# Third expert matrix in 16 KB runs, with an expert's hidden units dealt to the two halves in pairs

## The reference

```python
hdn = jax.nn.silu(xf @ w1[e]) * (xf @ w3[e])        # 1024 -> 512 hidden units
acc = acc + combine[:, e:e + 1] * (hdn @ w2[e])     # 512 -> 1024
```

## Time and profile before

| | |
|---|---|
| median of 3 runs | 716.95 us (716.07 to 717.56) |
| profiled execution, own time | 716.73 us |
| its span, first to last instruction | 715.0 us |
| PE busy | 609.8 us (85%) |
| weight loads (PEld) / DVE / ACT / POOL busy | 420.6 / 306.9 / 181.8 / 158.4 us |
| DMA traffic | 235.99 MB, mean 330 GB/s over the span |
| granted TensorE clock, mean | 0.961 |
| `into_hidden` (L694): matmul instructions | 1952 + 160, mean 396 and 407 ns |
| `down` (L715): matmul instructions | 464 + 64, mean 596 and 654 ns |
| issues of the expert matrices | 96 of 2048 KB |

### The profile page before, as it was taken

How to read it: one execution, slowest core, us unless ns; L and a number is a source line. 1 busy time by engine, 2 the same in 40 slices (tenths; PEclk the granted TensorE clock), 3 DMA queues, 4 the chain that set the end, 5 groups by cost and what they waited for, 6 DMA issues and landing times.

```text
span 715.0 us, 10596 instructions
## 1 busy us (share of the span) xinstructions
PE 609.8 (85%) x4220; PEld 420.6 (59%) x4220; DVE 306.9 (43%) x787; ACT 181.8 (25%) x287; POOL 158.4 (22%) x181
## 2 busy tenths in 40 slices
PE   5999999999999999889877987988788777877771
PEld 5999999878775556446444544554344435453440
DVE  4462485517577133353442353342434251433244
ACT  3323313302111313223232323322232121223130
POOL 1000000000000414244235224332341322233142
PEclk9999999999989999999999999899999999999996
DMA  9952133834496999999999999999999999999950
GB/s 250 282 184 90 45 118 105 339 135 190 152 392 250 390 418 420 417 416 417 422 416 421 413 422 416 422 416 421 422 418 421 415 422 420 425 415 418 404 223 21
DMA packets 45738, 235.99 MB, mean 330 GB/s; under 512 B 13667, under 2 KB 18275, under 8 KB 28712
## 3 DMA queue, kind: packets, MB, share of 16 engines
q1 hardware_dynamic: 32287, 220.92, 76.6%
q0 software_dynamic: 12544, 11.71, 4.9%
q10 hardware_dynamic: 857, 2.67, 0.9%
HBM read 237.69 MB, written 30.20 MB: 375 GB/s over the span
## 4 chain that ended last, share of the span: by engine, by line
PE 34%; issue 19%; DMA 17%; SPq 15%; POOL 9%; DVE 5%; ACT 1%; POOLq 0%; DVEq 0%; ACTq 0%
PE ps L534 14%; SPq L402 9%; PE ps L591 7%; DMA tenth_block<-in_w 6%; DMA blocks<-in_w 6%; PE ps L694 6%; SPq L406 5%; PE ps L715 2%; POOL out L1085 2%; POOL out L1081 2%; POOL prev L1077 2%; POOL first_outputs L1073 2%; DMA first_outputs<-ye,first_row 2%; DMA x_tok<-in_x_prompt 1%; DMA prev<-first_outputs,final_row 1%
## 5 line engine op out<-in xcount | busy, mean ns | idle before, releaser
L694 PE MATMUL ps<-blocks,ln 128*64 128x256 f32 x1952 | 233.5, 396 | 53.6 <-DMA blocks<-in_w 32.4
L694 PEld LDWEIGHTS ps<-blocks,ln 128*64 128x64 f32 x1952 | 157.0, 143 | 130.2 <-issue 57.2
L715 PE MATMUL ps<-blocks,hT 128*64 128x512 f32 x464 | 105.7, 596 | 6.0 <-DMA blocks<-in_w 5.8
L1077 POOL DMA_INDIRECT prev<-first_outputs,final_row x32 | 34.9, 1091 | 246.7 <-DMA first_outputs<-ye_more,first_row 119.3
L715 PEld LDWEIGHTS ps<-blocks,hT 128*64 128x64 f32 x464 | 32.8, 137 | 59.8 <-issue 48.5
L798 ACT ACTIVATE ln<-ps 128x512 f32<-128x512 f32 (+1 forms) x38 | 19.9, 572 | 112.2 <-PE ps L682 89.0
L1494 DVE SCALAR_TENSOR_TENSOR h_rows<-silu,slot_gate,ps 128x256 f32<-128x256 f32 x33 | 15.7, 477 | 69.0 <-PE ps L694 68.9
L1499 DVE COPY hT<-ps 128x256 f32<-128x256 f32 x33 | 13.9, 422 | 71.1 <-PE ps L703 71.1
L534 PE MATMUL ps<-xT_high,w_in_high 128*128 128x288 f32 x256 | 41.4, 305 | 0.9 <-DVE xT_low L1187 0.9
L981 ACT ACTIVATE std<-rstd,eps 128x1 f32<-128x1 f32 x32 | 9.4, 295 | 125.3 <-DVEq L1523 125.2
L534 PE MATMUL ps<-xT_low,w_in_high 128*128 128x288 f32 x256 | 39.5, 297 | 0.0
(11 more groups left out here) (232 smaller groups left out, 789.6 us busy)
## 6 DMA issues: line engine op xcount, KB each, us to landing
blocks<-in_w SPq DMA_DIRECT2D x87, 2048.0 KB, 36.5
tenth_block<-in_w SPq DMA_DIRECT2D x9, 2048.0 KB, 37.9
blocks<-in_w_in SPq DMA_DIRECT2D x3, 2048.0 KB, 10.5
blocks<-in_w_out SPq DMA_DIRECT2D x2, 2048.0 KB, 7.8
x_tok<-in_x_prompt SPq DMA_DIRECT2D x4, 512.0 KB, 5.2
blocks<-in_w_in SPq DMA_DIRECT2D x4, 512.0 KB, 11.3
first_outputs<-in_x_prompt SPq DMA_DIRECT2D x4, 512.0 KB, 8.7
x_rows<-x_tok ACTq DMA_DIRECT2D x4, 512.0 KB, 2.7
```

What stands on the lines that cost most here:

```text
L694: mm = pe.matmul(ps[64 * g:64 * g + 64, bank, 0:FH], x, w[:, k, g * FH:(g + 1) * FH], start=(k == 0), stop=(k == KD - 1))
L715: mm = pe.matmul(ps[64 * g:64 * g + 64, BY, :], hT[:, k % 2, k // 2 * SLOTS:(k // 2 + 1) * SLOTS], w[:, k, g * DH:(g + 1) * DH], start=(k ...
L1077: return g.indirect_dma_start(out=prev[w], out_offset=None, in_=first_rows[:, :], in_offset=rows_at(idx), bounds_check=last_row, oob_is_er ...
```

## The change

It has two sides that need each other. `load_out` gives partition p the rows 4p to 4p+3 of `w2`, one run of 16 KB. For these rows to meet their units, the 512 units are dealt to the halves by pairs: half g takes the units 4q + 2g and 4q + 2g + 1 for q = 0 to 127. In `into_hidden` the moving operand of half g is thus 128 pairs of neighbouring fp32 values, 8 bytes used and 8 bytes skipped, in place of 256 values in a row. What PE writes to PSUM, the number and order of all instructions, the transposes and `down` stay as they are, on every engine; SP has as many DMA issues as before.

```diff
@@ -403,8 +403,7 @@
             def load_out(b, e):
                 src = w2[e] if isinstance(e, int) else w2[bass.DynSlice(e, 1)].rearrange("e f d -> (e f) d")
-                sp.dma_start(out_block(b).rearrange("p (g c) d -> p g c d", g=2),
-                             src.rearrange("(g p c) d -> p g c d", g=2, c=KF // 2)).then_inc(block_loaded[b], 16)
+                sp.dma_start(out_block(b), src.rearrange("(p c) d -> p c d", c=KF)).then_inc(block_loaded[b], 16)
@@ -685,14 +684,14 @@
             def into_hidden(kind, b, loads, seq, i):
                 done, bank = (h1_done, B1) if kind == "w1" else (h_done, B3)
-                w = in_block(b)
+                w = in_block(b).rearrange("p k (q g c) -> p k g q c", g=2, c=2)
...
                     for g in range(2):
-                        mm = pe.matmul(ps[64 * g:64 * g + 64, bank, 0:FH], x, w[:, k, g * FH:(g + 1) * FH],
-                                       start=(k == 0), stop=(k == KD - 1))
+                        mm = pe.matmul(ps[64 * g:64 * g + 64, bank, 0:FH].rearrange("s (q c) -> s q c", c=2), x,
+                                       w[:, k, g, :, :], start=(k == 0), stop=(k == KD - 1))
```

## The result

| | before | changed |
|---|---|---|
| median, same chip, 7 runs each | 717.56 us | 721.97 us |
| range of the runs | 716.07 to 719.52 | 720.16 to 723.05 |
| ratio, 95% interval | | 1.0058 [1.0040, 1.0076] |
| profiled execution, own time | 716.73 us | 722.03 us |
| its span | 715.0 us | 720.3 us |

What follows compares the result with a forecast made beforehand. Block loads on the DMA engines were taken as the bound, the last `w3` landing setting the end: 716.73 - 2.4 (DMA) + 0 (PE) = 714.3, plus 0.2 for the median, 714.5 us; own range 713.3 to 715.3, 8 in 10 711.9 to 717.3.

Steps and rivals of the forecast that it cites:

- The failed step: POOL's gathers: small packets wait 0.3 us longer behind a 16 KB packet; taken as 0, 0.3 us at the end without cover.
- The chain over POOL is off the path: At the end, DVE waited 0.22 us for the last gather, the last `w2` having landed by then; cost taken as 0.
- 19.6 us for silu: Mid-kernel, PE's waits for ACT were said to come behind a late block, since silu uses what PE had just finished.
- 78 us are free: Expert part: PE busy 407.92 of 486 us, about 15 us unavoidable, so extra call time up to about 1 us fits.
- The DMA term: `w2` loads on the DMA engines: fewer, larger packets save 90 ns a load, 27 loads, 2.4 us; bounds 0 to 5.9.
- p = 0: `into_hidden` (L694): p is a call's extra time from gapped moving rows, taken as 0; upper end 3.4 us.
- the rival of a small p: L694 calls take 0.3 to 1 us longer, hidden in PE's gaps except 3p: 715.4 to 717.5 us; chance 0.07.
- The rival on the other side: L694 in every pair: gapped rows make PE the bound, near 880 us at half speed, 766 at p = 1.7; chance 0.11.

Runs made afterwards that it cites:

- gaps-only: Changed kernel with `w2` loaded as before in two runs of 8 KB, leaving only the gapped moving rows: 717.67 us, ratio 1.0012.
- DMA-only: Kernel before with only the changed `load_out` (`w2` in one 16 KB run), moving rows without gaps: 722.51 us, ratio 1.0083.
- all-8 KB: Kernel before with every `w1` and `w3` load also in two runs of 8 KB, no gaps: 720.34 us, ratio 1.0058.
- the round shortened: Kernel before with second norm one tile later and POOL's load of `prev` after store t, waiting only for store t-1: 721.90 us, ratio 1.0072.
- the fetch first: Changed kernel with POOL's fetch of a later pair's tokens issued ahead of the load of `prev`: 721.56 us, ratio 1.0078.
- later norm: Second norm of each tile handled one tile later: on the changed kernel ratio 1.0025, on the kernel before 0.9998, on DMA-only 1.0003.
- last edit: As the round shortened, but the last three tiles in the old order: changed kernel 1.0082, kernel before 0.9989, DMA-only 1.0061.
- late-tiles kernel: Kernel before with the whole change (16 KB `w2` runs, gapped rows) only from tile 20 on: 716.16 us, ratio 0.9981.

## Why the prediction was wrong, step by step

- **The failed step** is "A 16 KB packet holds its engine for 0.3 us longer, and the small packets of POOL's gathers wait behind it", with "The chain over POOL is off the path [...] I take 0". The mechanism was named, and priced once, at the end. But it acts all along the queue: 12.7 us in place of 11.5 for each store that POOL waits for, two a pair, and a pair was 29.2 us long instead of 27.1. Whether POOL was off the path was read from one row of the last 25 us; until 492 us PE ran at POOL's pace, and the earlier trace rows had shown it: its 19.6 us for silu were put down to late blocks. Cut at 485 us, that stretch has 17.9 of them, and no wait for a block, in its first part, and all of the 24.1 us for blocks in the second (below). The gaps-only, DMA-only and all-8 KB kernels show the step, the last of them in the other direction.
- **The spare time of PE.** "78 us are free" counted idle time as if it lay anywhere. The nine pairs up to 492 us need 51 loads, not 54, since the crowded expert's two tiles, 8 and 9, share one set of matrices (tile 9 is the added one, not the last tile, `E`). At 5.42 us a load these are 276 us, and at POOL's pace PE took them in 244: it won the 32 us by which it had begun behind the loads. The changed kernel begins some 3.5 us further behind (first `w1` of pair 1 at 252.4 instead of 248.4, the stream 0.5 later). Up to the last `w1` it needs 87 loads, 468 us at 5.38, and takes them in 438.1, so it wins 30: 6 us short by this estimate. Measured, the last `w3` was taken 456.6 us after the first issue, against 451.0 where PE kept up. More than half of the 6 us is thus the late start, in which PE waits 1.24 us for the fetch of pair 1 and then takes 5.35 us for a `down`. No run ties that to the packets: pair 1 begins 14.5 us behind the first issue, close to the 14.9 here, also with 8 KB packets and the round shortened, and 11.7 us behind it, near the 11.3 of before, in the changed kernel with the fetch first.
- **The DMA term** was right in mechanism and near in size: 2.4 us forecast at 90 ns a load, 3.0 to 3.2 measured, and 70 ns for loads in the other direction. By the prediction's own measure, landing to landing over 82 loads, a load took 5.38 us (5.377 to 5.385) in the four traces with 16 KB `w2` that have the landings (later norm and last edit, with and without gaps), and 5.42 (5.416 to 5.417) in three with 8 KB; forecast was 5.39. The Trainium skill's rule ("DMA: Bandwidth & Descriptors", section "Bandwidth") calls transfers under 64 KB descriptor-dominated; read to mean that 2 MB ones are not, it would have made the term 0. These runs show a gain at 2 MB a load, of about 2% of a load.
- **p = 0** was off by 0.18 us a call, less than the 0.3 us where the rival of a small p began. It cost the gaps-only kernel 0.9 us by its ratio, with an interval from 0 to 1.6. "SBUF — State Buffer", section "Specifications (TRN2)", of the Trainium skill says both that two hits a line give full bandwidth and that each cross to a new line costs. Here pairs cost 9 ns in 379 more, so the second half counted, and little.
- **The rival on the other side** (PE as the bound) didn't happen: PE is at 420.90 of 486 us. The true case, the pace of POOL's small transfers as the bound, was in none of the rivals.
- **What stays open.** A store lands 1.2 us later beside 16 KB packets, more than the 0.3 us of a single longer packet. It could be several such waits in a row, or a slower service of POOL's queue as a whole. The landings suggest that the delay adds up with what lies ahead in the queue. Medians from issue to landing, 260 to 640 us, with the later norm, 8 KB `w2` against the DMA half: the load of `prev`, which goes out when the store has landed, 8.3 and 8.4 us; the store 11.1 and 12.0; the two DMAs of a send 11.6 and 14.5, 13.1 and 16.0. With the last edit, where the load of `prev` goes out without waiting for the store just ahead, it takes 11.7 and 18.2 us (the rows above). So the wait for a store is how this kernel feels the change, but an order without that wait doesn't remove it. Which of the two mechanisms it is, no run separates. Nor has any kernel brought the whole 3 us to the end: shown is the earlier last `w3`, and in the late-tiles kernel 1.2 us (717.32 to 716.16) of total time, with an interval that ends close to 1.

PE's waits in the kernel before, from 330 to 485 us; the row for blocks of 485 to 640 us is that of the earlier trace rows, unchanged:

```profile
PE ps L694 <- ACT silu L939: 17.9, 6, 5.0
PE ps L703 <- DVE h_rows L1494: 2.4, 2, 1.6
PE ps L682 <- DMA ln<-x_rows,pair_row: 0.5, 1, 0.5
```

## What to carry to other kernels

Before calling an engine off the path, compare its round per tile (its instructions, gaps and waits summed) with the tile's period in each phase of the kernel, not its last wait. In this saturated DMA system a change of the big transfers' packet size also changed the latency of small transfers, most where several of them were queued; if a chain of small ones paces an early phase, try small packets there and larger ones only where the big stream is the limit. Idle time of an engine counts as spare only where nothing but that engine's own work would fill it; here a chain gathered it into waits of 5 us, which also cost clock.

## What the runs showed of the hardware

- An indirect store's way, from its issue until the load waiting for it was issued, took on the mean 8.5, 11.5 and 12.7 us beside a stream at full rate of 8 KB packets, a mixture, and 16 KB packets, though the 16 KB stream itself was the fastest (421 GB/s, against 419 for the mixture, in the earlier trace rows, and 416 for 8 KB).
- Of POOL's DMAs beside 16 KB packets, one that went out behind a drained queue landed after 8.4 us (median) instead of 8.3 beside the mixture, and those of a send after 14.5 and 16.0 instead of 11.6 and 13.1.
- A moving operand of fp32 pairs with gaps of 8 bytes cost 388 ns an instruction instead of 379, 5% on a whole call (3.85 against 3.67 us).
- After a wait of 4.63 us a call of 32 instructions took 5.44 us, and the next 3.85; after block waits of 1.4 us there was no such loss. The mean granted clock over 330 to 640 us fell from 0.95 to 0.93 though PE was idle for less of it (47.7 against 55.6 us); what differs is that the idle time lies in long waits: nine over 3 us, 37.8 us together, against two with 8.6.
